# Where the experts' down weights are loaded from: one queue or two, in a mixture-of-experts stage

## What is computed

```python
scores = sigmoid(xt @ router_w)
_, sel = top_k(scores + router_bias, 6)
wsel = take_along_axis(scores, sel); wsel = wsel / sum(wsel) * 2.5
for each expert e, over the tokens tok sent to it with weights wt:
    gu = xt[tok] @ w_gate_up[e]                  # 1024 -> 512
    h  = silu(gu[:, :256]) * gu[:, 256:]
    y  = (h @ w_down[e]) * wt                    # 256 -> 1024
routed = segment_sum of the y over the tokens
out = layer_norm(alpha * x + routed + shared expert)
```

## Time and profile before

| | us |
|---|---|
| median of 3 runs | 1322.85 (1322.81 to 1324.76) |
| the profiled execution, its own time | 1322.01 |
| its span, first to last instruction | 1319.7 |
| TensorE busy | 1241.5 (94%) |
| VectorE busy | 480.8 (36%) |
| ScalarE busy | 312.1 (24%) |
| GpSimd busy | 356.8 (27%) |
| bytes moved by the DMA engines | 312.82 MB, 237 GB/s on average |
| granted TensorE clock, mean | 0.98 of full speed |

### The profile page before, as it was taken

One profiled execution on the slowest core, in us unless ns is written; L12 is line 12 of the kernel. 1 busy time (PEld: TensorE's weight loads), 2 busy tenths in 40 slices (PEclk: granted clock), 3 DMA queues, 4 the chain that ended last, 5 costly groups with the idle time before them and its releaser, 6 DMA issues.

```text
span 1319.7 us, 23842 instructions
## 1 busy us (share of the span) xinstructions
PE 1241.5 (94%) x8589; PEld 782.5 (59%) x8590; DVE 480.8 (36%) x945; ACT 312.1 (24%) x829; POOL 356.8 (27%) x420
## 2 busy tenths in 40 slices
PE   8999999999999989999999899988899999988996
PEld 5587778777774458888557645444454455444442
DVE  3755665556514543233246511101111211111248
ACT  3332333323322442222133011111111011111111
POOL 2545535364602341000000232322122122322101
PEclk9999999999999999999999999988899999999998
DMA  4632333233023113435834399999999999999994
GB/s 131 188 96 86 119 111 122 62 110 111 16 64 121 49 36 93 112 103 168 348 129 158 127 406 418 421 419 423 421 418 423 411 412 392 382 427 423 424 405 196
DMA packets 119599, 312.82 MB, mean 237 GB/s; under 512 B 9774, under 2 KB 79534, under 8 KB 102992
## 3 DMA queue, kind: packets, MB, share of 16 engines
q1 hardware_dynamic: 106592, 284.53, 56.5%
q0 software_dynamic: 10768, 24.72, 5.0%
q10 hardware_dynamic: 2144, 2.22, 0.6%
HBM read 289.32 MB, written 34.38 MB: 245 GB/s over the span
## 4 chain that ended last, share of the span: by engine, by line
PE 46%; DMA 10%; DVE 4%; issue 2%; ACT 0%; SPq 0%; DVEq 0%; POOL 0%; POOLq 0%
PE bank L1990 17%; PE bank L1380 11%; PE bank L1997 8%; DMA expert_gu<-in_expert_w_gate_up_dram 7%; PE bank L1386 4%; PE bank L1982 2%; DVE x_rows L2277 1%; DMA late_rows<-choice_rows 1%; PE bank L2042 1%; PE bank L2066 1%; PE bank L1408 1%; DMA choice_rows<-expert_y,row_col 1%; PE bank L1401 1%; DVE x_rows L2288 0%; DMA gathered_x<-x_rows,tok_col 0%
## 5 line engine op out<-in xcount | busy, mean ns | idle before, releaser
L1990 PE MATMUL bank<-expert_gu,gathered_xT 128*64 128x256 f32 x2016 | 254.9, 406 | 27.7 <-DMA expert_gu<-in_expert_w_gate_up_dram 17.5
L1990 PEld LDWEIGHTS bank<-expert_gu,gathered_xT 128*64 128x64 f32 x2016 | 142.9, 140 | 120.4 <-issue 24.0
L2201 DVE SCALAR_TENSOR_TENSOR hidden<-gate,slot_w,bank 128x128 f32<-128x128 f32 x64 | 22.2, 348 | 399.5 <-ACT gate L2158 388.4
L1997 PE MATMUL bank<-expert_down,hiddenT 128*64 128x512 f32 x504 | 121.8, 603 | 2.5 <-issue 2.5
L486 PE MATMUL bank<-x_high,w_head_low 128*128 128x512 f32 x224 | 93.9, 419 | 0.0
L486 PE MATMUL bank<-x_high,w_head_high 128*128 128x512 f32 x224 | 93.3, 417 | 0.0
L486 PE MATMUL bank<-x_low,w_head_high 128*128 128x512 f32 x224 | 93.2, 416 | 0.0
L2158 ACT ACTIVATE gate<-bank 128x128 f32<-128x128 f32 x64 | 17.8, 278 | 274.3 <-PE bank L1990 274.3
L1885 POOL COPY row_col<-row_idx 128x1 int32 (+1 forms) x60 | 10.9, 181 | 257.5 <-ACT expert_y L2152 197.5
L1888 POOL DMA_INDIRECT choice_rows<-expert_y,row_col x60 | 59.9, 998 | 47.4 <-POOL row_col L1885 47.4
L676 POOL TENSOR_TENSOR w_head_low<-w_head,w_head_high 128x1024 fp32r<-128x1024 f32 x28 | 66.5, 2373 | 2.2
(11 more groups left out here) (397 smaller groups left out, 2256.6 us busy)
## 6 DMA issues: line engine op xcount, KB each, us to landing
expert_gu<-in_expert_w_gate_up_dram SPq DMA_DIRECT2D x63, 2048.0 KB
expert_down<-in_expert_w_down_dram SPq DMA_DIRECT2D x63, 1024.0 KB
w_head<-in_w_in_dram SPq DMA_DIRECT2D x32, 512.0 KB, 4.2
choice_rows<-zero_rows SPq DMA_DIRECT2D x6, 2048.0 KB, 9.2
late_rows<-choice_rows SPq DMA_DIRECT2D x4, 2048.0 KB, 21.2
w_tile<-in_w_in_dram SPq DMA_DIRECT2D x14, 512.0 KB, 4.0
x_rows<-in_x_dram SPq DMA_DIRECT2D x8, 512.0 KB, 6.6
first_rows<-choice_rows SPq DMA_DIRECT2D x4, 1024.0 KB, 18.0
```

Of the source, the lines that this page charges most:

```text
L1990: mm = nc.tensor.matmul(bank[parts[a], 0:2 * P], x[:, c, part], halves[:, a, :, :], start=(c == 0), stop=(c == KC - 1))
L1997: mm = nc.tensor.matmul(bank[parts[a], :], hidden_t[:, c * BLK:(c + 1) * BLK], dn[:, c, a * (D // 2):(a + 1) * (D // 2)], start=(c == 0), ...
```

## The change

SyncE's refill issues the gate/up loads alone. The down load of the slot that came free is issued by ScalarE, after the waits that stand ahead of its copy of the result and ahead of that copy. In step s, ScalarE has waited for the result of expert s-1 and loads the down weights of expert s+3 into the same slot. The first step loads none, and in the last turn steps 5 to 7 load none. The loads are the same 59 in number and size as before (experts 5 to 63), in the same order among themselves.

```diff
--- before.py
+++ after.py
@@ -1828,13 +1828,9 @@
 
     def sync(sp):
         def refill(i, slots):
-            for j in range(slots + 1):
-                if j < slots:
-                    k, now = (j + 1) % GROUP, (j + 1) // GROUP
-                    T["load_gu"](sp, j, GROUP * i + (j + 1), lambda: sp.wait_ge(h_psum[k], i + now))
-                if j:
-                    b, then_ = j % GROUP, j // GROUP
-                    T["load_down"](sp, j - 1, GROUP * i + j, lambda: sp.wait_ge(y_psum[b], i + then_))
+            for j in range(slots):
+                k, now = (j + 1) % GROUP, (j + 1) // GROUP
+                T["load_gu"](sp, j, GROUP * i + (j + 1), lambda: sp.wait_ge(h_psum[k], i + now))
 
         with sp.Fori(1, NE // GROUP - 1) as i:
             refill(i, GROUP)
@@ -2166,6 +2162,8 @@
                     act.wait_ge(y_psum[b], then_)
                     if not (first and s <= GROUP):
                         act.wait_ge(scattered[b], 16 * (then_ - 1))
+                    if not (first and s == 1) and not (last and s > GROUP):
+                        T["load_down"](act, (s - 2) % GROUP, STEPS * i + (s + GROUP - 1))
                     take_y(b, last and s > STEPS - DIRECT)
                 act.wait_ge(h_psum[k], now)
                 nc.scalar.copy(hT[:, k % 2, :], ps[4][:, k % 2 * P:k % 2 * P + P]).then_inc(ht_ready[k], 1)
```

## The result

The changed kernel takes 1350.09 us (median of 4 runs, 1347.23 to 1350.45), the kernel before 1322.83 in the same comparison: a ratio of 1.0204, 95% interval 1.0186 to 1.0223. It is 27 us slower. The forecast was 1327.0, in a range that ended at 1334.0: the direction was right, the size was not.

The account below looks back on a forecast made before the run. TensorE and the transfers were taken as nearly level, gate/up weights binding in the outer stretches. 2.5 us for one down load ahead plus 1.6 for a slow start made 4.1, so 1327.0 us, range 1320.0 to 1334.0.

Parts of the forecast that it names:

- the issues added on ScalarE: 59 issues ahead of ScalarE's copy of the result, plus a wait for the scatter of four steps ago: cost 0.
- a third queue now halves their turns: GpSimd's scatters get half their turns, and the first read-back waits for one: an added 2 us stays inside the range.
- SyncE's 59 issues gone: 59 down loads leave SyncE's queue, 20 us of issues over the stage; SyncE mostly waits, so nothing is gained.
- ScalarE's issue: Each down load's issue on ScalarE takes 0.4 us, 1.4 for the range, under 3.67 us of cover: cost 0.
- Rival 4: ScalarE blocks over 3.5 us on its issue because the engines' queues are full: 17 us at 4 us; chance 0.04.
- The law of turns: DMA engines alternate packets of 16 KB gate/up and 8 KB down, two to one; one down load gets ahead, 2.5 us.
- rival 1: Down loads go far ahead of gate/up at equal shares: 9.9 us, 12.2 with the low clock, 1332.8 to 1335; chance 0.2.
- The price of the two weights queues between themselves: One down load runs ahead of the gate/up load wanted first, so expert 57 starts 2.5 us later.
- one more slow start: One more short TensorE wait near the last experts, with products at the lower clock after it: 1.6 us, 0 to 2.3.
- Rival 2: Nothing moves: same bytes, full engines, order too little disturbed; 1322.85 within 2.6 us; chance 0.28.
- TensorE's waits for gate/up above 17.5 us: Sign that the forecast is right: TensorE waits longer for gate/up weights than the 17.5 us before.
- The rates of the outer stretches: Sign that the forecast is right: up to 1045 and from 1135 us, transfers at 415 to 422 GB/s, share still 1.01.

Follow-up runs that it names:

- one_act: Kernel before, with all gate/up and down refills issued by ScalarE at the end of its step, in one queue, none by SyncE: 1322.01 us, ratio 0.9994.
- two_16rows: Changed kernel, with each of the 60 block scatters cut to its first 16 of 128 rows, the output lacking the others: 1306.84 us, ratio 0.9877.
- one_16rows: Kernel before, with each of the 60 block scatters cut to its first 16 of 128 rows, the output lacking the others: 1304.56 us, ratio 0.9867.
- two_gu8_dn4: Changed kernel, with each gate/up load in two transfers of 8 KB runs and each down load in two of 4 KB: 1330.25 us; kernel before likewise, 1330.28.
- two_gu8: Changed kernel, with each gate/up load issued as two transfers with runs of 8 KB a partition instead of 16: 1333.35 us, ratio 1.0079.
- one_extra4: Kernel before, with four small extra loads a step, of 8 bytes a partition, in GpSimd's queue into unused memory: 1352.24 us, ratio 1.0212.

## Why the prediction was wrong

**The step that failed** is in the part on the issues added on ScalarE: "The load also gets a new wait, for the scatter of four steps ago: these land in 9.2 us, and four steps last some 30 us (the six from 1218.73 to 1266.39 took 47.7). Cost 0." The landing time was taken from the kernel before, for a queue whose share the change cuts. In the changed kernel it is 19.5 us (median) and 33.9 at most, as long as four steps and more, and ScalarE waited 80.5 us for scatters. The same holds for GpSimd's wait for each overflow scatter and for the read-back's wait. The text even says that "a third queue now halves their turns", and then gives it 2 us inside the range, without the division that belongs there: 9.5 packets an expert on each engine, at 0.92 us a round, is 8.7 us, and an expert lasts 8.57. The kernel before allowed an estimate of it: its weights' queue has 18 packets on each engine for an expert, GpSimd's some 9, so that two queues of 9 each leave nothing over. It cost some 20 to 25 us: 22.5 of difference with the packets left in, 2.3 with them out.

**What held, step by step.**
- SyncE's 59 issues gone: worth nothing, as said. one_act, which has none of SyncE's refills, is at 1322.01.
- ScalarE's issue: taken at 0.4 us, measured 0.35, 0.37 at most, and hidden. Rival 4 (ScalarE blocks on its issue) is out; what blocked it was the wait behind.

```profile
L2462 ACTq DMA_DIRECT2D expert_down<-in_expert_w_down_dram x59: 333/345/373, 768.6 to 1273.5; - x59
```

- The law of turns: "Taken in turn, packet by packet, that is two parts to one". 7.65 to 3.83 MB, at 522 and 524 packets, is 2.0 to 1. The rule of the Trainium skill ("DMA: Bandwidth & Descriptors", Queues, rings and completion order), that an engine goes round its queues a packet at a time, agrees to the packet where all three have work. The same page (SWDGE vs HWDGE vs iDMA) prefers packets of 4096 B at most, in its account of GpSimd's path. In GpSimd's queue the trace agrees, 4096 B is the largest; in the weights' queues it doesn't, 16384 and 8192 B, so rival 1's condition of equal packets isn't met. (The scatters, which the prediction took for 2 KB pieces, go in packets of two rows.)
- The price of the two weights queues between themselves, 2.5 us: two_16rows is 2.3 us above one_16rows, two_gu8_dn4 0.0 above its twin, and one down load ahead in one queue costs nothing that can be measured (1.0005). That is as forecast, but 2.3 us is no more than the intervals of the two runs leave open. Whether the 1.6 us for one more slow start came can't be told.
- Rival 1 had the wrong reason for a loss over 9.9 us: TensorE did not wait longer for gate/up. Its sign in the list of checks, a lower rate in the middle stretch, did appear, at 356 GB/s, from the other cause.
- Rival 2, that the time stays, fails by the clearest margin. The Trainium skill ("DMA: Bandwidth & Descriptors", Issuing engines are not separate DMA queues) has several issuing engines save only the issue time. The transfers do interleave on the same engines, but with a share for each queue, and that share is what changed.
- "TensorE's waits for gate/up above 17.5 us" was wrong, 4.4: TensorE was held up elsewhere first, so the weights were there. The rates of the outer stretches, forecast at 415 to 422 GB/s, were 407 and 414.

**Left open.** Whether two_gu8's 9.3 us are order or its lower rate. How the 17.2 us of the stage divide between waits and slow starts after them was not measured apart. How much of one_extra4's 28 us is GpSimd's own time for the issues isn't known. No version with the whole output is measurably faster than the kernel before.

## What to carry to other kernels

Before a transfer is moved to a queue of its own, count the packets of every queue that shares the engines, not their bytes. Here a queue got one packet a round (522, 524 and 524), and the added queue made the round longer by its own packet. The queue that pays is the one with many small packets, and who waits for it may be an engine that the change never touches. A landing time read from the trace holds for the old number of queues. Before it is used as cover, compare the turns that the queue needs with those that the new round leaves it: here 9.2 us became 19.5, and 33.9 at most.

## What the runs showed of the hardware

- With all three queues full the DMA engines serve them one packet each: 522, 524 and 524 in 30 us; two queues stand at 969 and 974 (one_extra4).
- The landing time of a transfer grows with that: a block scatter took 9.2 us (median) beside one weights queue and 19.5 beside two, with the same bytes in all.
- A contiguous run of 16 KB on each partition is one packet of its own, so is one of 8 KB, and a row of 4 KB in a gather. In a scatter two rows of 2 KB share a packet (112 rows fewer are 48 packets fewer: four less one on each of 16 engines). Pieces of 8 to 32 bytes are packed eight to a packet, and each transfer on all 16 engines has 16 packets of 4 bytes more (144 for a weight load of 128 runs, 32 for 128 small pieces). These small packets take turns too.
- Rows that a scatter drops for their index still take their packets (10768 with and without the drop).
- Runs of 4 KB for the down weights, with 8 KB for gate/up, come with 412 GB/s with the engines full (share 1.02) instead of 419 (1.01), and with 7 us more on 1323.
